# Another order of the first mixer's tiles in a two-block float32 network on one core

## What is computed

```python
h = rms_norm(x, g_mix)
proj = h @ w_in                                  # 1280 LRU, 1024 pool, 2048 gate columns
xa = depthwise_conv(u_a, conv_a_w, conv_a_b, 2)  # 4 taps, 10 heads of 128
r = sigmoid(block_diag(xa, wa, ba)); i = sigmoid(block_diag(xa, wx, bx))   # per direction
log_a = -8.0 * r * softplus(-lam)
b_in = sqrt(-expm1(2.0 * log_a)) * (i * xa)
h_dir = scan(exp(log_a), b_in)                   # forward and backward
y_a = (h_fwd + h_bwd) @ p_a
pooled = window_mean(u_b, w) - u_b               # w = 2, 4, 8, 16, 256 channels each
y_b = (block_diag(pooled, w_pool, b_pool) * pool_scale) @ p_b
merged = gates_a * y_a + gates_b * y_b
x = x + merged @ w_out
x = x + (gelu(up_1) * up_2) @ w_down             # up = conv3(rms_norm(x) @ w_up)
x = rms_norm(x, g_final)
...                                              # second block: S5, sparse attention, gated FFN
u = rms_norm_2(h, norm1_g) * (1.0 + scale1) + shift1
xs, q, ckv, ... = split(u @ w_in_2)
```

## Time and profile before

| | |
|---|---|
| median of 3 runs | 1592.31 us |
| the profiled execution: its time, its span | 1593.16 us, 1591.9 us |
| granted TensorE clock, mean | 0.984 |
| TensorE matmul busy | 1530.5 us (96%) |
| VectorE, ScalarE, GpSimd busy | 843.0, 835.4, 281.7 us |
| DMA, mean | 207 GB/s |

### The profile page before, as it was taken

One profiled execution on the slowest core, in us unless ns is written; L12 is line 12 of the kernel. 1 busy time (PEld: TensorE's weight loads), 2 busy tenths in 40 slices (PEclk: granted clock), 3 DMA queues, 4 the chain that ended last, 5 costly groups with the idle time before them and its releaser, 6 DMA issues.

```text
span 1591.9 us, 17748 instructions
## 1 busy us (share of the span) xinstructions
PE 1530.5 (96%) x6632; PEld 1195.6 (75%) x6632; DVE 843.0 (53%) x1627; ACT 835.4 (52%) x1066; POOL 281.7 (18%) x308
## 2 busy tenths in 40 slices
PE   6899999999999999999989999879999999999997
PEld 5687788788788888888767666546877888888886
DVE  6778634564487766544445999897654121111011
ACT  5678877844555555544445435742545444444431
POOL 2111111111111111111112123222311111111110
PEclk9999999999999999999999999989999999999999
DMA  8667777799899989899979678344987998888872
GB/s 259 158 151 185 196 185 181 179 313 311 253 243 254 229 198 217 240 268 234 223 187 246 174 208 224 111 139 138 296 229 174 248 227 187 195 183 198 185 173 79
DMA packets 99221, 329.37 MB, mean 207 GB/s; under 512 B 11568, under 2 KB 13104, under 8 KB 99008
## 3 DMA queue, kind: packets, MB, share of 16 engines
q0 software_dynamic: 36704, 133.56, 44.2%
q1 hardware_dynamic: 58320, 186.81, 35.2%
q10 hardware_dynamic: 4112, 7.87, 1.3%
HBM read 179.69 MB, written 18.87 MB: 125 GB/s over the span
## 4 chain that ended last, share of the span: by engine, by line
PE 74%; DVE 14%; ACT 6%; issue 2%; DMA 1%; POOL 1%; SPq 1%; ACTq 0%; DVEq 0%; POOLq 0%
PE ps L725 24%; PE ps L726 24%; PE ps L728 24%; DVE sml L1994 2%; DVE pl_f L1997 2%; DVE pl_f L1943 1%; DVE pl_f L1790 1%; ACT whi L1106 1%; ACT wlo L1115 1%; DVE pl_f L1945 1%; ACT pl_f L1200 1%; DVE pl_r L1510 1%; SPq L2392 1%; PE ps L799 1%; DVE pl_f L1594 1%
## 5 line engine op out<-in xcount | busy, mean ns | idle before, releaser
L725 PE MATMUL ps<-pl_r,whi 128*128 128x512 f32 x1976 | 788.7, 399 | 23.4 <-DVE pl_f L1594 7.7
L726 PE MATMUL ps<-pl_r,wlo 128*128 128x512 f32 x1976 | 783.8, 397 | 0.0
L728 PE MATMUL ps<-pl_r,whi 128*128 128x512 f32 x1976 | 783.7, 397 | 0.0
L725 PEld LDWEIGHTS ps<-pl_r,whi 128*128 128x128 f32 x1976 | 372.9, 189 | 125.0 <-issue 15.5
L728 PEld LDWEIGHTS ps<-pl_r,whi 128*128 128x128 f32 x1976 | 372.7, 189 | 92.4 <-DVE pl_r L1526 1.1
L726 PEld LDWEIGHTS ps<-pl_r,wlo 128*128 128x128 f32 x1976 | 373.2, 189 | 89.3 <-issue 0.5
L2162 POOL DMA_DIRECT2D wlo<-raw x238 | 206.3, 868 | 1109.6 <-ACT wlo L1115 1084.6
L1106 ACT ACTIVATE whi<-raw 128x1024 fp32r<-128x1024 f32 x247 | 260.1, 1053 | 205.1 <-PE ps L728 168.8
L1115 ACT ACTIVATE wlo<-raw 128x1024 fp32r<-128x1024 f32 x238 | 249.0, 1046 | 0.0
L2134 DVE TENSOR_TENSOR pl_f<-ps,pl_f 128x512 f32<-128x512 f32 x22 | 15.2, 692 | 177.5 <-PE ps L728 177.5
L1510 DVE TENSOR_TENSOR pl_r<-pl_f,pl_r 128x512 fp32r<-128x512 f32 x120 | 83.1, 692 | 49.1 <-ACT pl_r L1135 32.8
(11 more groups left out here) (226 smaller groups left out, 1206.4 us busy)
## 6 DMA issues: line engine op xcount, KB each, us to landing
raw<-in_w SPq DMA_DIRECT2D x245, 512.0 KB, 5.2
wlo<-raw POOLq DMA_DIRECT2D x238, 512.0 KB, 6.3
pl_f<-in_mod SPq DMA_DIRECT2D x48, 512.0 KB, 7.4
tab<-pl_f SPq DMA_DIRECT2D x16, 512.0 KB, 6.9
pl_f<-tab POOLq DMA_DIRECT2D x16, 512.0 KB, 6.2
xs<-pl_f SPq DMA_DIRECT2D x16, 256.0 KB, 7.5
pl_f<-xs SPq DMA_DIRECT2D x16, 256.0 KB, 7.1
spill<-pl_f ACTq DMA_DIRECT2D x16, 256.0 KB, 3.9
```

Source lines behind the costliest of these rows:

```text
L725: matmul(out, wh, sr(pair, kk, "hi"), start=start, stop=False)
L726: matmul(out, wl, sr(pair, kk, "hi"), start=False, stop=False)
L728: mm = matmul(out, wh, sr(pair, kk, "lo"), start=False, stop=stop)
```

## The change

Only the list is made otherwise; no function and no operation changes. As the table is 13 lines shorter, every line of the new file below it has a number lower by 13.

```diff
+PARTS = {"p": "pool", "i": "lru_in", "l": "lru", "m": "pmix", "b": "bb", "g": "ga"}
+_count = dict.fromkeys(PARTS, 0)
 MIX = []
-_work = [("pool", t) for t in range(8)] + [("pmix", t) for t in range(8)] + [("bb", m) for m in range(8)]
-_ga = 0
-for _i, (_n, _g) in enumerate(zip((2, 2, 2, 2, 4, 4, 2, 2, 2, 1, 1), (0, 1, 1, 1, 1, 1, 1, 1, 0, 0, 0))):
...
-assert not _work and _ga == 7
+for _c in "ipgpipilgpplgppilpgimmlmmgimmmlmgiblibblbbgilbilblb":
+    MIX.append((PARTS[_c], _count[_c]))
+    _count[_c] += 1
```

## The result

The changed kernel takes **1583.69 us** (median of 5 runs, 1581.82 to 1586.15) against 1592.31 us for the kernel before in the same session (5 runs, 1590.02 to 1596.56). The ratio is **0.9935, 95% interval 0.9921 to 0.9949**: 0.5 to 0.8% faster, or 8.6 us by the medians. The prediction was 1582.0 us, range 1578.0 to 1588.5, with 0.82 on faster by over 0.3%. Of the two profiled executions the one after takes 1582.71 us against 1593.16, which is 10.45 us less; the forecast's sum was 10.3.

What follows compares the result with a forecast made beforehand. TensorE was taken as the bound, busy 96% of the span, leaving only its waits and slow clock to win. Mixer 3.2 plus copies 7.1 gave 10.3 us, 1582.9 against the profiled execution, 1582.0 at the median; range 1578 to 1588.5.

Steps and rivals of the forecast that it cites:

- The bound: Whole kernel: TensorE's matmuls busy 96% of the span, so an order can win only its waits and the slow clock.
- Term 2: Second block's first norm: u on new places no longer waits for the copies that stack wst; 7.1 us.
- Rival 2: Gain at the copies does not last, a wait elsewhere takes its place; 3.2 us in all, 1589.1 us, chance 0.10.
- Term 1: First mixer: i1 and i2 ahead of l0 remove the wait at 64.86; 3.2 us of the 8.2 lost.
- the walk of VectorE: First mixer: VectorE's queue timed item by item; l1 ends at 102.6, 3.2 us earlier, i4's taps at 139.6.
- The stop at i3: First mixer: TensorE waits 3.2 us until 104 for the low half of the unit that i3 begins with.
- The clock at 139.6: First mixer, behind the 3.4 us wait for i4's bank: no clock fall counted; one would cost 2.1 us.
- rival 1: The mixer gives little: clock falls at 139.6 (1584.1 us) or VectorE reaches i4 no earlier (1585.2 us); chance 0.20.
- TensorE has no slack up to g5: First mixer behind i4's bank: a clock fall at 139.6 would cost its 2.1 us in the open.
- here the order gains: First mixer at l1: i2 long done, sigmoids start right behind p4's copy; l1 ends 3.2 us earlier.
- The clock rule: Skill's rule that repeated TensorE waits restart each group at the low clock; by it the sum would be 8.2 us.
- Rivals 3 and 4: No change, neither wait on the path: 1592.3 us, 0.06; slower, 1.2 GHz from g4 through i6: 1608 us, 0.02.

Runs made afterwards that it cites:

- the places alone: Against the kernel before: work in the old order, memory places handed out by the new order; 1584.57 us against 1593.03, ratio 0.9954.
- the order alone: Against the kernel before: work in the new order, memory places handed out by the old order; 1589.96 us against 1593.03, ratio 0.9983.
- u alone moved: Against the kernel before: only u takes the lowest free run from place 33 on, off bt's places; 1586.21 us against 1593.03, ratio 0.9962.
- the gates ahead: Against the changed kernel: gate tiles g4 ahead of i4, g5 ahead of i5, g6 behind i5; 1578.79 us, ratio 0.9901 to the kernel before.
- i1 alone ahead: Against the old order with the new places: one swap, i1 ahead of p2; 1582.48 us, ratio 0.9938 to the kernel before.
- l2 behind p7: Against the changed kernel: l2 moved two items, from ahead of p7 to behind g3; 1594.91 us, ratio 1.0000 to the kernel before.
- i2 ahead: Old order, new places, i2 ahead of l0, l1 still behind p4: 1582.66 us; also with g4, g5 ahead of i4, i5, g6 behind m7: 1579.50 us.

## Why the prediction was right

**The bound.** That an order can only win TensorE's waits and the clock behind them held: its busy time and waits account for the whole difference, and the two places named, the mixer and the copies, carry 3.25 and 7.1 of 10.3 us.

**Term 2, 7.1 us.** It measured 7.1 in the change, 7.1 with the places alone, -0.1 with the order alone, and 8.0 with u alone moved (7.1 of them from u's first matmul on). Every step stood: tile 0's wait, tiles 2.2 us apart, full clock. The table's first load (old L2196) was issued at 805.52, where I had said about 809, and held nobody. Rival 2 fell.

**Term 1, 3.2 us.** The size was right (3.25 at A) and so was the walk of VectorE, to 0.3 us over 75 us of program. Three steps in it were off, and two of them nearly cancelled, which is luck and no merit of the walk.

- *The stop at i3.* Forecast 3.2 us until 104, measured 1.86 us until 102.96: the 5.9 us of flight of the low half was taken as a bound from above, and was one.
- *The clock at 139.6.* I took none. It did fall: from 141.32 on the matmuls are 0.63 us and more (granted clock 0.50 from 141.40 to 144.00). The stretch from m3's first matmul to the 13th behind it (139.41 to 144.37) took 4.96 us, and the same stretch before (142.82 to 146.47) 3.65 at full clock, with the same short bank stop in it. So the clock cost 1.3 us here, less than rival 1's 2.1.
- *"TensorE has no slack up to g5".* This was wrong, and it is why the loss hardly shows. Before, TensorE also stopped for a moment at three banks behind m3, each stop about 0.5 us from start to start more than the cadence:

```profile
144.74 0.50 PE L725 MATMUL ps<-pl_r,whi 128*128 128x512 f32 x1 [0.25 <-DVE pl_f L1644]
163.44 0.50 PE L725 MATMUL ps<-pl_r,whi 128*128 128x512 f32 x1 [0.24 <-DVE pl_f L1594]
165.35 0.50 PE L725 MATMUL ps<-pl_r,whi 128*128 128x512 f32 x1 [0.25 <-DVE pl_f L1644]
```

VectorE was the bound up to i5, not up to m3. The first of these stops is there in the change too (at 141.32). The other two, at i5's bank and its neighbour's, are gone: late by the clock, TensorE finds those banks free and gets 1.0 us back. Matmul by matmul, its lead over before is 3.4 us at m3 (139.41), 2.1 at 144.37 and 3.1 at 162.56. The experiment with the gates ahead shows the same from the other side: with the stop at m3 and its clock gone the counted stretch gains 7.7 us in place of 3.3.

**Where the credit was misplaced.** The words "here the order gains: ... l1's sigmoids waited on ScalarE for i2's tile" are right, but I gave the gain to i2's new place alone and took TensorE's wait at 64.86 for a symptom that only shifts. The run with i1 alone ahead shows that the wait was a cause as well: it made i2's tile late, which made ScalarE and then VectorE late. Had the change had only that swap, I would have forecast 2 to 3 us too little.

**The clock rule.** The change's trace shows the half clock behind waits of 1.86 and 2.47 us. The Trainium skill, "TensorE: Matmul & The Clock Gate", section "HAM oscillation — how this bites in real kernels", describes a loop in which TensorE waits for a DMA in front of every group and starts each group at the low clock. The trace agrees that the low clock comes behind both new stops, though at the second one only behind six matmuls at full clock. The sum that I had made with that rule (8.2 us) was still too low by 2, as the fall cost 1.3 us and not 2.1, and 1.0 of it came back. But a stop does not always bring it, as the last section shows.

**Rivals.** Rival 1's clock fell where it said and cost 1.3 us, 0.3 net. Rivals 3 and 4 have nothing for them: the low clock behind 139.41 lasted 3 us, not 57. (Rival 4's own figure was off: its 44 blocks are 132 matmuls, which at 12 in 4.96 us take 54.6 us.)

## What to carry to other kernels

A list that sets the order of the work and also feeds a walk over memory places has two effects, and the second can be the larger and far away: here 7.1 of 10.3 us came 650 us behind the edit, and moving one item by two positions lost them again. Give each its own input before judging either, and look for tiles whose new owner waits for a DMA that reads the old one.

When TensorE waits for the bank of an engine that is the bound of a stretch, moving that engine's items around each other moves every bank that it frees, so follow each of those tiles before you do it: the change gained 3.3 us that way, two further reorderings of the heads lost 3 to 4. Surer here was to put work there that the engine has no part in; three gate tiles moved ahead gave 3 to 5 us more.

A wait that "only shifts" may still feed back: follow it through the other engines once around before calling it free.

## What the runs showed of the hardware

The granted clock does not follow from the length of one wait. These two stops are at the same matmul, i3's first, with the same releaser. In the kernel with the gates ahead the clock falls behind 1.87 us (granted clock 0.50 from 103.30 to 106.60, matmuls 0.43 us apart); in the one with l2 behind p7 it does not, behind 1.85 us:

```profile
102.31 0.47 PE L712 MATMUL ps<-pl_r,whi 128*128 128x512 f32 x1 [1.85 <-DMA wlo<-raw]
```

whose next matmuls follow at the full cadence of 0.234 us from the second on (granted clock 1.00 from 102.40 to 110.00). Stops of 1.80 and 1.82 us near 110 (the two kernels with i2 ahead) brought no half clock either, one of 1.83 us near 111 did (i1 ahead, from 112.58 on), and those of 2.0 to 2.5 us at 139 did in all four kernels that have them, about 2 us after the stop's end and not at once. A price for a short stop should be given with and without the clock: against the full cadence the half clock cost 1.3 to 1.6 us behind these short stops, and 1.6 to 2.6 us behind the stops of 4.8 to 9.8 us.

The half clock behind a stop lasted 7 to 14 matmuls in all of these runs, 14 behind 9.77 us, and was full again by itself while TensorE went on.
